# A hybrid attention and ConvGLU layer on one core: the forget scan, two stores, a weight sum and a down weight in other places

## What is computed

```python
(aq, ak, av, bq, bk, bv, cq, ck, cv, ciq, cik, ciw, dq, dk, dv, df) = split(x @ w_in)
# C: indexer; each query keeps its 256 best keys
score[t, s] = sum_h ciw[t, h] * relu(ciq[t, h] . cik[s] * 64 ** -0.5)
# D: forgetting attention, a cumulative sum over the tokens
c = cumsum(log_sigmoid(df + b_forget))
logits_d[t, s] = dq[t] . dk[s] / 8 + c[t] - c[s]
gates = sigmoid(x @ w_gate + b_gate)
x1 = layer_norm(alpha * x + sum_n(gates[n] * (o[n] @ w_branch[n])) @ w_out)
a = conv_b + causal_conv3(x1 @ w_up, conv_w)
y = layer_norm(alpha * x1 + (gelu(a) * (x1 @ w_ffn_gate)) @ w_down)
```

## Time and profile before

| | |
|---|---|
| median of 3 runs | 2074.19 us (2074.11 to 2074.42) |
| profiled execution, its own time | 2075.71 us |
| its span in the profile | 2073.9 us |
| mean granted TensorE clock | 0.998 of full |
| busy: PE, PEld | 2050.6 us (99%), 1718.8 us (83%) |
| busy: DVE, ACT, POOL | 1542.0 us (74%), 988.2 us (48%), 969.2 us (47%) |
| PE's share of the chain that ended last | 89% |

### The profile page before, as it was taken

How to read it: one execution, slowest core, us unless ns; L and a number is a source line. 1 busy time by engine, 2 the same in 40 slices (tenths; PEclk the granted TensorE clock), 3 DMA queues, 4 the chain that set the end, 5 groups by cost and what they waited for, 6 DMA issues and landing times.

```text
span 2073.9 us, 29066 instructions
## 1 busy us (share of the span) xinstructions
PE 2050.6 (99%) x10346; PEld 1718.8 (83%) x10346; DVE 1542.0 (74%) x2571; ACT 988.2 (48%) x1779; POOL 969.2 (47%) x824
## 2 busy tenths in 40 slices
PE   9999999999999999999999999999999999999998
PEld 7788888888888888888888888888788888888887
DVE  8679998677677666688786666768877777775668
ACT  5543333366563565654755666423433433344540
POOL 4287776133332332234533333625765556555651
PEclk9999999999999999999999999999999999999999
DMA  4233333310105111132022000431666655558862
GB/s 133 72 112 103 110 112 102 62 31 21 31 11 193 42 51 42 41 122 73 30 72 82 21 21 13 157 146 62 190 199 182 205 178 174 161 195 312 279 208 92
DMA packets 199103, 230.57 MB, mean 111 GB/s; under 512 B 25896, under 2 KB 149800, under 8 KB 198960
## 3 DMA queue, kind: packets, MB, share of 16 engines
q1 hardware_dynamic: 196048, 218.72, 33.9%
q10 hardware_dynamic: 2912, 10.00, 1.3%
HBM read 167.31 MB, written 61.37 MB: 110 GB/s over the span
## 4 chain that ended last, share of the span: by engine, by line
PE 89%; DVE 4%; issue 2%; POOL 1%; ACT 1%; DMA 1%; SPq 0%; ACTq 0%; DVEq 0%
PE pair L951 14%; PE pair L1387 14%; PE pair L1251 9%; PE obank L1387 6%; PE obank L1045 5%; PE pair L935 5%; PE chunk L1024 5%; PE pair L1416 4%; PE pair L1346 4%; PE obank L1251 4%; PE pair L996 3%; PE pair L997 3%; PE pair L1297 2%; PE chunk L1416 2%; PE obank L1416 2%
## 5 line engine op out<-in xcount | busy, mean ns | idle before, releaser
L2244 POOL TENSOR_TENSOR w_lo<-w_raw,w_hi 128x1024 fp32r<-128x1024 f32 x58 | 148.2, 2556 | 257.1 <-ACT w_hi L1692 257.1
L1715 ACT ACTIVATE pt_hi<-chunk 128x512 fp32r<-128x512 f32 (+1 forms) x272 | 150.6, 554 | 167.2 <-PE chunk L1024 165.2
L2661 DVE TENSOR_TENSOR pt_lo<-chunk,pt_hi 128x512 fp32r<-128x512 f32 (+1 forms) x272 | 173.4, 638 | 75.4 <-ACT pt_hi L1715 69.7
L2299 POOL TENSOR_SCALAR prob<-prob,att 128x256 f32<-128x256 f32 (+4 forms) x172 | 120.5, 709 | 192.1 <-DVE att L2597 191.9
L951 PE MATMUL pair<-act_hi,w_hi 128*128 128x512 f32 x432 | 186.3, 431 | 0.8 <-DVE heads L2602 0.5
L951 PE MATMUL pair<-act_hi,w_lo 128*128 128x512 f32 x432 | 169.9, 393 | 0.0
L951 PE MATMUL pair<-act_lo,w_hi 128*128 128x512 f32 x432 | 169.3, 392 | 0.0
L2477 DVE TENSOR_SCALAR_CACHE_REDUCE o_top<-score,stat 128x384 uint8<-128x384 f32 (+1 forms) x186 | 167.5, 942 | 0.7
L1045 PE MATMUL obank<-pt_hi,heads 128*128 128x256 f32 (+1 forms) x568 | 148.6, 285 | 0.9 <-DVE pt_lo L2661 0.9
L1045 PE MATMUL obank<-pt_lo,heads 128*128 128x256 f32 (+1 forms) x568 | 138.1, 280 | 0.0
L1824 ACT ACTIVATE prob<-prob,att 128x257 f32<-128x257 f32 (+6 forms) x172 | 120.6, 702 | 35.0 <-DVE att L2587 33.7
(11 more groups left out here) (491 smaller groups left out, 6031.2 us busy)
## 6 DMA issues: line engine op xcount, KB each, us to landing
down_sums<-dn_sums SPq DMA_DIRECT2D x40, 512.0 KB, 6.1
w_raw<-in_w_in SPq DMA_DIRECT2D x33, 512.0 KB, 4.7
w_raw<-in_w_gate SPq DMA_DIRECT2D x22, 512.0 KB, 5.0
gates<-o_t SPq DMA_DIRECT2D x22, 512.0 KB, 3.2
up_raw<-in_w_up SPq DMA_DIRECT2D x22, 512.0 KB, 4.8
gate_raw<-in_w_ffn_gate SPq DMA_DIRECT2D x22, 512.0 KB, 6.0
hidden<-gelu_s SPq DMA_DIRECT2D x22, 512.0 KB, 3.3
dn_raw<-down_sums SPq DMA_DIRECT2D x44, 256.0 KB, 4.0
```

Source lines behind the costliest of these rows:

```text
L1715: nc.scalar.activation(dst, src, func, **kw).then_inc(act_part, 1)
L2299: nc.gpsimd.tensor_scalar(prob_slot(br, u)[:, 0:n], prob_slot(br, u)[:, 0:n], att_stat(3, u), 1.0, ALU.mult, ALU.mult).then_inc(prob_ready, 1)
L2661: nc.vector.tensor_tensor(pt_lo[:, n % PT_SLOTS, 0:m], t[:, 0:m], pt_hi[:, n % PT_SLOTS, 0:m].bitcast(F32), ALU.subtract).then_inc(chunk_f ...
```

## The change

It has four parts.

1. VectorE runs the scan behind the low parts of `iq 0` (`forget_scan`, a function of its own), no longer ahead of them. The store of the forget sums, with its wait for the scan, leaves ScalarE's block and stands in SyncE's at the head of the stage `scores`.
2. The store of the first filler's gate tile leaves ScalarE's block. SyncE issues it, with the wait for the sigmoid, between the first two loads of the stage `gates`.
3. In `up`, tile 0: the weight sum (1, 7) is made behind the combination of (0, 5) instead of ahead of it.
4. In `down`: ScalarE splits down weight 12 ahead of hidden tile 15 instead of behind it.

```diff
@@ SyncE
                 if step[0] == "scores":
+                    sp.wait_ge(forget_set, 2)
+                    sp.dma_start(c_dram, prob[F_AT:P, 0, :]).then_inc(c_stored, 16)
                     sp.dma_start(gate_bias[:, :], b_gate[0].rearrange("(c p) -> p c", p=P),
                                  allow_slow_non_contiguous=True).then_inc(late_params, 16)
...
                     for k in range(2):
                         sp.wait_ge(lo_ready, ring_at["gates",] - 1 + k)
                         load_gate_raw(0, k)
+                        if k == 0:
+                            sp.wait_ge(filler_taken, 1)
+                            sp.dma_start(gates_dram[FILLER_GATES[0]], bias).then_inc(filler_stored[0], 16)
@@ ScalarE
                 nc.scalar.activation(buf, src[:, :], ACT.Sigmoid, bias=gate_bias_of(*FILLER_GATES[i])).then_inc(filler_taken, 1)
-                act.wait_ge(filler_taken, i + 1)
-                act.dma_start(gates_dram[FILLER_GATES[i]], buf).then_inc(filler_stored[i], 16)
+                if i > 0:
+                    act.wait_ge(filler_taken, i + 1)
+                    act.dma_start(gates_dram[FILLER_GATES[i]], buf).then_inc(filler_stored[i], 16)
...
-                    if step[1] == 0:
-                        act.wait_ge(forget_set, 2)
-                        act.dma_start(c_dram, prob[F_AT:P, 0, :]).then_inc(c_stored, 16)
...
-                    for n in range(4, H_OPS):
+                    for n in range(4, H_OPS - 1):
...
                         if n + DN_SLOTS < NDOWN:
                             split_down(n + DN_SLOTS)
+                        if n == 0:
+                            split_h(H_OPS - 1)
@@ VectorE
                 own(nc.vector.scalar_tensor_tensor(z, z, 0.0, az, ALU.min, ALU.subtract))
+
+            def forget_scan():
+                z, az, ones = prob[F_ROWS, 1, :], prob[F_ROWS, 0, :], bias[F_ROWS, :]
                 nc.vector.tensor_tensor_scan(az, ones, z, 0.0, ALU.mult, ALU.add).then_inc(forget_set, 1)
...
                     last.then_inc(pair_free[k], 1)
+                    if step[1] == 0:
+                        forget_scan()
...
                             combine(n, p, up_s[:, HALF:SEQ], first, place)
-                            weight_sums(q + OP_AHEAD + 1)
+                            weight_sums(q + OP_AHEAD + (n > 0))
...
-                        if (n, p) != (0, 4):
+                        if (n, p) not in ((0, 6), (0, 4)):
                             weight_sums(q + OP_AHEAD + 1)
```

## The result

| | before | with the change |
|---|---|---|
| median on the same chip | 2074.45 us (6 runs, 2074.11 to 2074.87) | 2086.44 us (6 runs, 2085.76 to 2087.41) |
| ratio, 95% interval | | 1.0056 [1.0045, 1.0067] |
| profiled execution, its span | 2075.71 us, 2073.9 us | 2085.76 us, 2083.9 us |
| mean granted clock | 0.998 | 0.996 |

The account below looks back on a forecast made before the run. TensorE, busy 2050.6 of 2073.9 us, bounds the kernel, so only its standstills count. 11.6 + 1.8 - 0.45 - 0.8 - 0.33 = +11.8 us gives a median of 2086.0 us, range 2082.5 to 2089.

Parts of the forecast that it names:

- filler load held: more standstill: SyncE's wait for the scan delays the first filler weight's load, so TensorE stands still 11.6 us more.
- low clock behind it: After the long stop, the first filler matmuls run at 1.2 GHz, losing 1.8 us.
- edit 2, ReLU: ScalarE's ReLU follows the filler's sigmoid without the store between, cutting TensorE's wait at 75.5 us: -0.45 us.
- edit 3, combination: In up, the (0,5) combination no longer waits behind a weight sum, removing TensorE's stop at 1454 us: -0.8 us.
- edit 4, down weight: In down, the earlier weight split readies its low part sooner, removing TensorE's stop at 1889 us: -0.33 us.
- Rival 1: Filler weight's load lands in 4.1 us instead of 6.8, the bias's packets being done early: 2083.3 us; chance 0.12.
- rival 2: No low clock after TensorE's stop at the first filler: 2084.2 us; chance 0.06.
- rival 3: Load starts after the bias lands, or the low clock lasts twice as long: 2087.8 to 2090 us; chance 0.15.
- rival 4: Filler load not held, the scan ending before it is needed; small gains stand alone: 2072.3 us; chance 0.03.
- One sign: TensorE's standstill at 54 us would be 11 to 13 us, longer than all its other waits together.
- the first half of edit 1: On VectorE, the scan behind the first indexer tile's low parts lets the first filler start at most 0.3 us sooner.
- rival 5: Change does not do what it says: wait met at once, or small gains lost behind, 2087.6 us; chance 0.1.

Follow-up runs that it names:

- the warm TensorE: The changed kernel with 45 extra matmuls ahead of the first filler, their results overwritten by it; 2084.13 us, ratio 1.0044.
- edits 2 to 4 alone: The kernel before with the filler store on SyncE, the later weight sum and the earlier down weight split, scan and store unmoved; 2072.62 us, ratio 0.9989.
- the repeat: The whole change unaltered, run again against the kernel before; 2085.48 us, ratio 1.0054.
- edit 1 alone: The kernel before with only the scan behind the low parts and its store on SyncE; ratio 1.0069, run again 2087.76 us, ratio 1.0066.

## Why the prediction was right, and where it was not

The median was put at 2086.0 us and is 2086.44. I compare intervals, since the profile after is 1.15 us ahead at the log-sigmoid (47.29 against 48.44), far before any edit.

| term | predicted | measured |
|---|---|---|
| filler load held: more standstill | +11.6 | +11.0 (11.45 - 0.48) |
| low clock behind it | +1.8 | +1.84 |
| edit 2, ReLU | -0.45 | -0.63 |
| edit 3, combination | -0.8 | -0.90 |
| edit 4, down weight | -0.33 | -0.35 |
| sum | +11.8 | +10.93 |

The clock and edit 2 come from one interval, from the first filler matmul to the first of the third filler, `chunk<-act_hi,w_hi`. It is 38.97 us before, 40.18 after, 38.34 with the warm TensorE and 38.33 with edits 2 to 4 alone. So edit 2 gives 0.63 (38.97 less 38.34) and the clock takes 1.84 (40.18 less 38.34). Edit 3 is 27.01 us before and 26.11 after, between the two `pair<-t,op_late` that are released by `t` and by the last `gate_s`. Edit 4 is 199.32 before and 198.97 after, from the first `pair<-dn_more,act_hi` to the last matmul of `down`. The profiled spans differ by 10.0, which is the sum less the 1.15 us at the start, plus 0.2 us elsewhere. The medians differ by 12.0 in the first comparison and by 10.95 in the repeat, so the total is known to about a microsecond and no better. That the forecast came within 0.4 us of the first median is therefore in part luck: its sum is 0.9 us above that of the trace, with a hold 0.6 us too long and small gains 0.3 us too small.

**The held load, point by point.** The scan ended 6.03 us after the last log-sigmoid operation began; the earlier trace rows and the new order had given 6.06 (54.5 - 48.44). The bias's issue took 0.39 us, not 0.58, the row of 14.54 us. The load behind it landed in 6.5 us, 6.8 predicted; the choice between 4.1 and 6.8 was right, and the run with the bias ahead shows that both ends are real (4.2 us there). From ScalarE's split to the first filler matmul it took 3.63 us, against 4.05 before (50.48 to 54.53), where VectorE was the last to be ready; the prediction had 3.7: GpSimd's operation ran 2.35 us rather than 2.55, as no scan was beside it. Rival 1 (a landing in 4.1 us), rival 2 (no low clock), rival 3 (a longer hold) and rival 4 (no hold) are all out. The scores waited for nothing more, as predicted. One sign did not come: the standstill was to be longer than all other waits of TensorE together, and it is 11.4 us against 12.4.

**The step that failed** is the first half of edit 1, the scan behind the low parts "at most 0.3 us" in gain and without a cost. In the change that cannot be seen, because GpSimd's operation comes more than 8 us after the scan. Where the load isn't held, the scan's move gives the 0.45 us of the first filler and costs a stop of 0.94 us, or 2.40 us with the store on ScalarE. The prediction took the scan's 2.29 us, from a row in which the scan had begun before GpSimd, for its duration in any place. The rows that held the warning were in view: operations of one shape from 0.67 to 1.78 us, beside a busy GpSimd. They were weighed for edit 3 and not for edit 1. The forecast did not suffer, as the hold covered it; the expectation for the version with the store behind the loads did, by 0.8 to 1.1 us, about the 0.94 us of this stop.

**Edit 3** gave 0.90 us although a part of it went to a wait behind, as rival 5 has it. The matmuls of (0, 3) start 0.96 us sooner (2.72 us behind the start of the matmuls ahead of them instead of 3.68), 0.32 us came back at the next combination, and a gap of about 0.2 us at 1466 us went as well. The moved weight sum took 1.18 us and its follower 1.78.

**The version with the lowest median** has the scan in its old place, the store in SyncE's block behind the second filler load, and edits 2 to 4: 2072.43 us, 2.4 us below the kernel before. Edits 2 to 4 alone have 2072.62 us, and from the transposes to the third filler 39.82 us against 39.85, so the store's place is worth nothing that shows.

## What to carry to other kernels

A wait put into an engine's queue holds all that is behind it: list those instructions with the times at which they are issued now, and a load that goes out 30 us early is the first to look at, since nothing in the profile before marked it as needed. When a loss of 12 us is undone, look at the trace again for what it covered; here a second, smaller loss of the same edit stood behind it. A duration belongs to its neighbourhood: before an operation of VectorE moves, see what GpSimd does at the new time.

## What was unexpected of the hardware

**VectorE's scan beside GpSimd.** With the same data and shape it took 2.29 us in nine traces where GpSimd was idle as it began, and 3.97 and 3.96 us in the two where GpSimd's `w_lo` had begun 0.57 us earlier. In both it ended 2.15 us after GpSimd's operation did (52.80 to 54.95, 53.48 to 55.63), nearly the 2.29 us of a whole scan, as if it had only begun then. ScalarE is not the cause, since with the store on ScalarE it did nothing from 51.02 us until the scan's end at 55.63, nor are transfers, since none moved data from 50 to 54 us in either run. The other way round, that `w_lo` took 2.54 or 2.55 us in the three traces where it began while the scan ran, against 2.34 to 2.37 in the six where it began long after. The low parts `iq_t<-pair,iq_t` kept 1.24 us each beside the same GpSimd operation; they read one operand from PSUM, the scan both from SBUF. The Trainium skill (SBUF — State Buffer, section Who interferes with whom) has just this rule: a VectorE instruction with two SBUF inputs contends with a GpSimd one that reads SBUF, and the later one is blocked until the first is done. These traces agree with it for the scan. For GpSimd's operation they agree in part: it began 0.37 us before the scan's end and took some 0.2 us longer, and not the whole 0.37. I made no run with the scan and GpSimd alone.

The weight sums of `up`, which also read both operands from SBUF, show the same in many places. Here is one of the shape and operands that took 1.66 us in the earlier trace rows, with the two operations of GpSimd around it:

```profile
1466.69 0.69 DVE L2788 SCALAR_TENSOR_TENSOR w_sum<-w_sum,up_raw 128x512 f32<-128x512 f32 x1
```

```profile
1461.92 2.27 POOL L2254 TENSOR_TENSOR op_late<-up_raw,op_late 128x512 fp32r<-128x512 f32 x1
1468.13 1.54 POOL L2254 TENSOR_TENSOR op_late<-w_sum,op_late 128x512 fp32r<-128x512 f32 x1 [3.94 <-ACT op_late L1732]
```

The kernel before has 90 single rows of `w_sum` between 1420 and 1860 us. The 23 with no operation of GpSimd beside them took 0.68 or 0.69 us each, the 67 that began while one ran took 0.85 to 1.79. The combination `gate_s<-first_s,obank` reads one operand from PSUM and took 0.67 us beside a busy GpSimd.

**The clock's loss varies with the execution.** The stop of 8.92 us in the run with only the wait cost 2.57 us at the low clock (41.54 us over the interval above, against 38.97), that of 11.45 us in the change 1.84, in its repeat 1.56 behind 11.57, and in edit 1 alone 1.49 behind 11.90. With the bias ahead of the wait it is 1.76 us behind 8.65 (40.10 us against 38.34), so two stops of nearly the same length, 8.65 and 8.92 us, have losses 0.8 us apart. So the length of the stop does not give the loss. The matmuls began at 1.2 GHz in all five, and the time until 2.4 GHz was back differed.

**The same load lands at different speeds.** `gate_bias`, 16 KB in single elements, took 7.2 us to land at 14.5 us and 4.2 us at 53.7. Around the first the DMA engines moved 369 GB/s, ahead of the second nothing; that this is the reason was not tested. The load of 0.5 MB behind it took 6.8 and 6.5 us, with 2.78 and 2.47 us in the issue alone.
